# A streaming encoder layer on one core: tile 0 routed first, and the convolution shared by three engines

## The chip, the cores and the metric

The kernel runs on one core of a Trainium2 chip. The metric is the device time of one execution in microseconds (us), the median of several runs. A profiled execution is timed on its own, and its trace gives the rows below.

## What is computed

One layer over 512 prompt frames and 32 sample frames, width 1024, all in float32. The reference, cut:

```python
z = rmsnorm(x) @ w_in                       # columns: q | k | v | gate g | conv a | conv b
q, k = rotary(q), rotary(k)                 # 4 heads of 128
o, state = retention(q, k, v, state)        # decayed scores, running state
y_ret = silu(g) * groupnorm(o)
u = a * sigmoid(b)
c = depthwise_conv31(concat(conv_buf, u))   # 512 channels, 31 taps
y_conv = silu(layernorm(c))
x = x + concat(y_ret, y_conv) @ w_out
h = rmsnorm(x)
for head in range(8):                       # product-key experts
    s = (h @ query) @ keys                  # 2 x 128 scores
    e, best = top16_of_sums(top16(s1), top16(s2))
    x += sum_k softmax(best)[k] * gelu(h . down[e_k]) * up[e_k]
y = rmsnorm(x)
```

## The kernel before

**Tiles.** The 544 frames are five tiles: 0 to 3 of 128 prompt frames, tile 4 the 32 sample frames (`SAMPLE`). The kernel has a front (norm, projections, convolution, retention, output projection) and then the expert stage. In that stage each of 34 units (a tile and a head; `vt`) gathers 16 rows per frame: one gather brings 128 rows of 8 KB, 1.05 MB, into one of 11 slots. VectorE multiplies the first half with the frame and sums (`weigh`), ScalarE makes the gelu, the weight and a diagonal matrix of it, and PE adds diagonal times second half into PSUM (`sum_up`); four rows form a group, so `sums(vt, g)` are 16 matmul instructions. When PE has used a slot, the next gather may fill it. There are 34 x 16 = 544 gathers.

**Where the slots lie.** The 11 slots share their memory with the ring of three weight sections (512 columns each) and with `z`, which holds the projections. So a slot opens only when the weights or rows in it are no longer needed.

**Names of PE's jobs.** Q(t), K(t), V(t), G(t): projection of tile t on queries, keys, values, gate (`qkvg`), 16 matmul instructions at 128x512 each. `glu`: the two halves of the convolution's input, channels on partitions, four chunks of 128 channels. `head(t)`: transposes of the rotated q and k (`ret_qT`, `ret_kT`). `scores(t)`: q times k. `out(t)`, `state(t)`: scores times values, and the new state. `back(t)`: transpose of the normed result (`ret_yT`). `ln_mean`, `ln_var`: channel sums of the convolution for its layer norm. `mix_out(t, i)`: half i of the output projection. `ffn_t`, `query`, `keys`: transposes, query and key product of head 0. The lists `JOBS` and `TRANSITION` are PE's order, written out by hand; each job takes the next PSUM bank, and the engine that empties it counts on a semaphore.

**The other engines** run lists in program order too. An instruction that waits holds all behind it on its engine. On VectorE (line L728) the convolution is 31 rounds, one per tap, over four channel chunks, with one instruction for 512 prompt frames and one for 32 sample frames each, and a drain behind each round:

```python
for src, lo, n in ((u_p, 0, SEQ), (u_s, SEQ, DEC)):
    out = conv[:, c, lo:lo + n]
    ...
            last = v.scalar_tensor_tensor(out=out, in0=src[:, c, j:j + n], scalar=tap, in1=out,
                                          op0=ALU.mult, op1=ALU.add)
```

GpSimd makes the rotary (L441 to L444: 12 operations of 256 columns per tile), the decayed keys (L451), the inverse roots of the norms (L408, L414; `retention_root(t)` is the one that the retention norm of tile t needs) and issues the gathers (L465):

```python
mixed_root(0)
mixed_root(1)
pool.wait_ge(s_idx, 1)
gathers(0, 0, 3)
mixed_root(2)
pool.wait_ge(s_wsec, len(WEIGHT_ORDER) - 2)
gathers(0, 3, 7)
mixed_root(3)
pool.wait_ge(s_wsec, len(WEIGHT_ORDER))
gathers(0, 7, SLOTS)
```

SyncE's queue loads inputs, weight sections (2 MB each) and head weights, and stores the results.

## Time and profile before

| | |
|---|---|
| Median of 3 runs (lowest, highest) | 1795.74 us (1795.22, 1797.34) |
| Profiled execution | 1796.54 us, span 1794.6 us |
| PE busy | 1522.6 us, 85% |
| VectorE (DVE) busy | 1171.6 us, 65% |
| GpSimd (POOL) busy | 744.8 us, 42% |
| ScalarE (ACT) busy | 496.4 us, 28% |
| Gathers' queue | 570.46 MB, 77.1% of 16 DMA engines' span |

The span is the time from the first to the last instruction. Busy shares are means over the front and the expert stage, which have different limits, so they are read by stretches below. PE executes each float32 matmul as two rows of the trace.

### The profile page before, as it was taken

How to read it: one execution, taken by the hardware profiler on the slowest of the kernel's cores; microseconds unless marked ns; L12 is line 12 of the kernel's file. 1: busy time of each engine (PE TensorE's matmuls, PEld its weight loads, DVE VectorE, ACT ScalarE, POOL GpSimd, SP SyncE). 2: the span in 40 equal slices, each digit the busy share in tenths (PEclk: the TensorE clock that was granted, in tenths of full speed). 3: DMA queues.
4: the chain of work that ended last, by engine and by line, in shares of the span. 5: the costliest groups of instructions: out<-in, count | busy, mean ns of one | idle time of the engine just before them, and what ended most of it. 6: DMA issues, size and time to landing. Idle time of an engine off the chain costs nothing.

```text
span 1794.6 us, 14135 instructions
## 1 busy us (share of the span) xinstructions
PE 1522.6 (85%) x4008; PEld 700.3 (39%) x4008; DVE 1171.6 (65%) x2667; ACT 496.4 (28%) x1562; POOL 744.8 (42%) x654
## 2 busy tenths in 40 slices
PE   7999979968988978997798889788977988777887
PEld 3544345534433433342244334333423443332332
DVE  2089863357567767766766777677677677777655
ACT  1000110122332333332333323333333332333332
POOL 1002144133254545453554544444454445455452
PEclk9899989989999999998999999999999999899899
DMA  5112100288999999999999999999999999999996
GB/s 221 47 58 83 62 1 1 68 341 329 362 404 421 421 421 421 422 421 422 421 402 423 422 420 401 422 421 389 408 422 421 421 421 422 421 421 410 421 416 248
DMA packets 84847, 605.53 MB, mean 337 GB/s; under 512 B 10880, under 2 KB 11136, under 8 KB 13088
## 3 DMA queue, kind: packets, MB, share of 16 engines
q0 software_dynamic: 78336, 570.46, 77.1%
q1 hardware_dynamic: 6432, 34.16, 5.0%
q8 instruction: 32, 0.52, 0.1%
q14 instruction: 47, 0.39, 0.1%
HBM read 601.31 MB, written 2.88 MB: 337 GB/s over the span
## 4 chain that ended last, share of the span: by engine, by line
DMA 39%; PE 38%; DVE 13%; ACT 4%; issue 2%; POOL 1%; DVEq 1%; ACTq 1%; POOLq 0%; SPq 0%
DMA arena<-experts,expert 38%; PE ps L1246 21%; DVE region_b L728 6%; PE ps L1217 5%; PE ps L1090 5%; DVE arena L933 5%; PE ps L1077 3%; ACT weight L623 2%; ACT diag L630 1%; PE ps L1082 1%; PE ps L1189 1%; POOL arena L465 1%; PE ps L1104 1%; ACT gl L620 1%; ACTq L625 1%
## 5 line engine op out<-in xcount | busy, mean ns | idle before, releaser
L1246 PE MATMUL ps<-arena,diag 128*128 128x512 f32 x2176 | 1031.2, 631 | 234.1 <-ACT diag L630 233.9
L465 POOL DMA_INDIRECT arena<-experts,expert x544 | 669.3, 1230 | 760.3 <-PE ps L1246 672.4
L933 DVE CUSTOM_DVE_ANT_0 arena<-arena,hn 128x1024 f32<-128x1024 f32 x544 | 654.8, 1222 | 365.9 <-DMA arena<-experts,expert 361.4
L1246 PEld LDWEIGHTS ps<-arena,diag 128*128 128x128 f32 x2176 | 428.8, 201 | 818.9 <-issue 603.4
L620 ACT ACTIVATE gl<-dots 128x4 f32<-128x4 f32 x136 | 27.9, 205 | 801.4 <-DVE dots L933 801.4
L630 ACT ACTIVATE diag<-cst,weight 128x128 f32<-128x128 f32 x544 | 173.8, 390 | 9.6 <-issue 0.3
L1090 PE MATMUL ps<-arena,hT 128*128 128x512 f32 (+1 forms) x320 | 145.9, 616 | 1.0 <-issue 1.0
L623 ACT ACTIVATE weight<-gl,gate 128x1 f32<-128x1 f32 x544 | 115.8, 283 | 9.9 <-issue 0.7
L728 DVE SCALAR_TENSOR_TENSOR region_b<-region_b,par 128x512 f32<-128x512 f32 x240 | 108.0, 521 | 2.7 <-issue 0.5
L1217 PE MATMUL ps<-hT,region_b 128*128 128x512 f32 x224 | 98.5, 593 | 0.4 <-issue 0.4
L441 POOL TENSOR_TENSOR hn<-arena,cst 128x256 f32<-128x256 f32 (+1 forms) x20 | 16.2, 808 | 193.5 <-ACT arena L529 127.0
L1090 PEld LDWEIGHTS ps<-arena,hT 128*128 128x128 f32 (+1 forms) x320 | 56.9, 181 | 86.8 <-issue 86.8
L1090 PE MATMUL ps<-arena,region_b 128*128 128x512 f32 (+1 forms) x160 | 70.5, 594 | 0.0
L1217 PEld LDWEIGHTS ps<-hT,region_b 128*128 128x128 f32 x224 | 42.5, 190 | 53.5 <-issue 53.5
L1077 PE MATMUL ps<-hT,arena 128*128 128x512 f32 x128 | 58.5, 619 | 2.8 <-DVE hT L707 2.5
L713 DVE SCALAR_TENSOR_TENSOR region_b<-region_b 128x512 f32<-128x512 f32 x4 | 2.5, 686 | 75.8 <-ACT region_b L517 75.8
L944 DVE TENSOR_TENSOR xs<-ps,xs 128x1024 f32<-128x1024 f32 (+1 forms) x34 | 41.4, 1219 | 15.3 <-PE ps L1246 15.3
L933 DVE DVE_READ_ACCUMULATOR2_ANT dots<- 128x1 f32 x544 | 44.5, 82 | 0.0
L620 ACT ACT_TABLE_LOAD x34 | 43.6, 1283 | 0.6
L606 ACT ACT_TABLE_LOAD x33 | 42.3, 1283 | 1.7
L1090 PEld LDWEIGHTS ps<-arena,region_b 128*128 128x128 f32 (+1 forms) x160 | 27.0, 174 | 36.8 <-issue 36.5
L529 ACT ACTIVATE arena<-ps 128x512 f32<-128x512 f32 (+1 forms) x15 | 8.9, 595 | 110.7 <-PE ps L1090 110.7
...
## 6 DMA issues: line engine op xcount, KB each, us to landing
arena<-weights SPq DMA_DIRECT2D x8, 2048.0 KB, 8.9
region_b<-head_weights SPq DMA_DIRECT2D x8, 1152.0 KB, 9.4
arena<-experts,expert POOLq DMA_INDIRECT x544, 14.9
...
```

Source lines behind the costliest of these rows:

```text
L465: pool.indirect_dma_start(rows_of(n), None, experts, bass.IndirectOffsetOnAxis(ap=expert[:, vt % BUFS, k:k + 1], axis=0))\
L606: nc.scalar.activation(gate[:, u, :], best_s[:, u, :], ACT.Exp, bias=neg_max[:, u:u + 1], accum_out=gate_sum[:, u:u + 1]).then_inc(s_exp, 1)
L620: nc.scalar.activation(gl[:, vt % 2, ks], dots[:, vt % 2, ks], ACT.Gelu_apprx_tanh)
L623: nc.scalar.activation(weight[:, vt % 2, k:k + 1], gl[:, vt % 2, k:k + 1], ACT.Copy, scale=gate[:, vt % BUFS, k:k + 1])
L630: nc.scalar.activation(diag[:, n % DIAGS, :], base, ACT.Copy, scale=weight[:, vt % 2, k:k + 1])\
L728: last = v.scalar_tensor_tensor(out=out, in0=src[:, c, j:j + n], scalar=tap, in1=out, op0=ALU.mult, op1=ALU.add)
L933: last = v.tensor_tensor_reduce(out=rows_of(n)[:, 0:D], in0=rows_of(n)[:, 0:D], in1=hn[:, tile_of(vt)], scale=1.0, scalar=0.0, op0=ALU.mul ...
L944: v.tensor_tensor(out=xs[0:rows, tile], in0=total, in1=xs[0:rows, tile], op=ALU.add).then_inc(s_acc, 1)
L1077: last = mm(out, w[:, k, c * P:(c + 1) * P], hT[:, k, 0:SEQ], start=k == 0, stop=k == KD - 1)
L1090: last = mm(out[0:r, :], lhs[:, k, lo:lo + r], w[:, k, :], start=k == 0, stop=k == KD - 1)
L1217: last = mm(out, weights[:, k, i * KEYS:(i + 1) * KEYS], hT[:, k, 0:SEQ], start=k == 0, stop=k == KD - 1)
L1246: last = mm(ps[:, 2 * (vt % 2) + half, :], diag[:, n % DIAGS, :], rows_of(n)[:, D + half * SEC:D + (half + 1) * SEC], start=k == 0, stop=k ...
```

## The change

1. **PE's order** is one list (`plan()`). Q comes first, then GLU in 16 halves of 272 frames. Tile 0 is taken through keys, gate, values, retention and output projection ahead of the others; values, retention and output projections of tiles 1 to 4 stand between tile 0's expert work.
2. **Convolution.** Prompt and sample frames lie in one row of 574 columns per channel chunk (`WIDE`), so a tap is one instruction. VectorE does chunks 0 and 1 in 31 rounds, then tile 0's gate and scores, then chunk 2. Chunk 3 (`POOLED`) is done by ScalarE (`products`: input times tap, three buffers) and GpSimd (`tap_sums`: 30 additions).
3. **Rotary** works in place on q and k together, 6 operations of 512 columns per tile.
4. **Layer norm** of the convolution in two blocks, frames 0 to 127 first. Copies of the retention's transposes move from VectorE to ScalarE.
5. **Gathers** of unit 0 are issued one by one as memory comes free, with a slot table (`SLOT`); the first slots are reused before the others are free. Eight PSUM banks in place of seven.

```diff
-WEIGHT_ORDER = [S_A, S_B, S_Q, S_K, S_G, S_V, S_OUT, S_OUT + 1]
+WEIGHT_ORDER = [S_Q, S_A, S_B, S_K, S_G, S_V, S_OUT, S_OUT + 1]
...
+    order = turn("norm_t", 0) + turn("norm_t", 1) + rows(S_Q, 0) + turn("norm_t", 2) + rows(S_Q, 1)
+    order += turn("norm_t", 3) + rows(S_Q, 2) + turn("norm_t", SAMPLE) + rows(S_Q, 3, SAMPLE)
+    order += [("glu", s, c, i) for s in (S_A, S_B) for c in range(CT) for i in range(2)]
+    order += rows(S_K, 0) + rows(S_G, 0) + rows(S_V, 0) + head(0) + rows(S_K, 1) + scores(0) + rows(S_K, 2) + out(0)
+    order += rows(S_K, 3, SAMPLE) + rows(S_G, 1) + back(0) + rows(S_G, 2) + blocks("ln_mean") + rows(S_G, 3)
+    order += blocks("ln_var") + rows(S_G, SAMPLE) + mix(0, 0) + mix(0, 1) + rows(S_V, 1) + head(1) + turn("ffn_t", 0)
+    order += scores(1) + query(0) + keys(0) + out(1) + rows(S_V, 2, 3, SAMPLE) + back(1) + head(2) + mix(1, 0)
+    order += scores(2) + mix(1, 1) + out(2) + head(3) + back(2) + scores(3) + turn("ffn_t", 1) + out(3) + query(1)
+    order += sums(0, 0) + keys(1) + head(4) + back(3) + scores(4) + mix(2, 0) + out(4) + mix(2, 1) + back(4)
+    order += mix(3, 0) + sums(0, 1) + turn("ffn_t", 2) + mix(3, 1) + query(2) + mix(4, 0) + keys(2) + turn("ffn_t", 3)
+    order += sums(0, 2) + mix(4, 1) + query(3) + sums(0, 3) + keys(3) + turn("ffn_t", 4) + sums(1, 0) + query(4)
+    return order + sums(1, 1) + keys(4)
...
+OPENING = [0, 1, 2, 3, 4, 5, 6, 0, 1, 2, 3, 7, 8, 9, 10]
+CYCLE = [4, 5, 6, 0, 1, 2, 3, 7, 8, 9, 10]
+SLOT = OPENING + [CYCLE[n % SLOTS] for n in range(VT * TOPK - len(OPENING))]
```

SyncE's queue, the part with the output weights:

```diff
+            sp.wait_ge(s_pe, JOB[("qkvg", S_K, SAMPLE)] + 1)
+            weight_rows(S_OUT)
+            sp.wait_ge(s_convout, 32)
+            sp.wait_ge(s_conv, 1)
+            sp.wait_ge(s_pooled, TAPS - 1)
             sp.dma_start(head_flat[0], head_weights[0]).then_inc(s_hw[0], 16)
+            sp.wait_ge(s_pe, JOB[("qkvg", S_G, SAMPLE)] + 1)
+            weight_rows(S_OUT + 1)
+            sp.wait_ge(s_rot, TILES)
+            sp.dma_start(first_gain, gain_ffn.to_broadcast([P, D])).then_inc(s_gain1, 16)
+            sp.wait_ge(s_yconv, len(BLOCKS))
```

GpSimd:

```diff
+            def tap_sums(lo, hi):
+
+                for j in range(lo, hi):
+                    pool.wait_ge(s_product, j)
+                    if j == 1:
+                        pool.wait_ge(s_tap, 1)
+                    else:
+                        pool.wait_ge(s_pooled, j - 1)
+                    nc.gpsimd.tensor_tensor(out=conv[:, POOLED, :], in0=conv[:, POOLED, :],
+                                            in1=tap_product[:, j % TEMPS, :], op=ALU.add).then_inc(s_pooled, 1)
...
+            pool.wait_ge(s_cst, 16)
+            tap_sums(1, 7)
+            rotary(0)
+            decayed_keys(0)
+            tap_sums(7, TAPS)
+            retention_root(0)
+            rotary(1)
+            decayed_keys(1)
+            for t in range(2, TILES):
+                rotary(t)
 
...
             mixed_root(0)
+            pool.wait_ge(s_idx, 1)
+            pool.wait_ge(s_gate, TILES)
+            gathers(0, 0, 1)
+            retention_root(1)
+            decayed_keys(2)
+            pool.wait_ge(s_pe, JOB[("qkvg", S_V, SAMPLE)] + 1)
+            gathers(0, 1, 3)
+            pool.wait_ge(s_pe, JOB[("ret_yT", 1)] + 1)
+            gathers(0, 3, 4)
             mixed_root(1)
-            pool.wait_ge(s_idx, 1)
-            gathers(0, 0, 3)
+            retention_root(2)
+            decayed_keys(3)
+            pool.wait_ge(s_pe, JOB[("ret_yT", 2)] + 1)
+            gathers(0, 4, 5)
+            retention_root(3)
+            decayed_keys(4)
+            pool.wait_ge(s_pe, JOB[("ret_yT", 3)] + 1)
+            gathers(0, 5, 6)
+            retention_root(4)
             mixed_root(2)
-            pool.wait_ge(s_wsec, len(WEIGHT_ORDER) - 2)
-            gathers(0, 3, 7)
+            pool.wait_ge(s_pe, JOB[("ret_yT", 4)] + 1)
+            gathers(0, 6, 11)
             mixed_root(3)
-            pool.wait_ge(s_wsec, len(WEIGHT_ORDER))
-            gathers(0, 7, SLOTS)
+            pool.wait_ge(s_pe, JOB[("mix_out", SAMPLE, 0)] + 1)
```

ScalarE:

```diff
+            def products(lo, hi):
+                for j in range(lo, hi):
+                    if j > TEMPS:
+                        act.wait_ge(s_pooled, j - TEMPS)
+                    tap = G_TAPS + POOLED * TAPS + j
+                    nc.scalar.activation(tap_product[:, j % TEMPS, :], u[:, POOLED, j:j + WIDE], ACT.Copy,
+                                         scale=par[:, tap:tap + 1]).then_inc(s_product, 1)
...
+            act.wait_ge(s_u, 1)
+            products(1, 6)
+            rows_in(S_K, 0)
+            products(6, 10)
+            rows_in(S_G, 0)
+            products(10, 14)
             rows_in(S_V, 0)
-            act.wait_ge(s_by["dve"], EMPTIED[("ln_mean", 1)])
-            for c in range(CT):
-                nc.scalar.activation(yT[:, HEADS + c, :], conv[:, c, :], ACT.Square).then_inc(s_csq, 1)
-            rows_in(S_V, 1)
-            act.wait_ge(s_by["dve"], EMPTIED[("ln_var", 1)])
-            nc.scalar.activation(deviation, var[:, :], ACT.Sqrt).then_inc(s_dev, 1)
-            rows_in(S_V, 2)
-            act.wait_ge(s_yh, 1)
-            for c in range(CT):
-                nc.scalar.activation(yT[:, HEADS + c, :], conv[:, c, :], ACT.Tanh).then_inc(s_yt, 1)
-            rows_in(S_V, 3)
-            rows_in(S_V, 4)
+            turned_heads(0)
+            products(14, 18)
```

VectorE:

```diff
+            dve.wait_ge(s_st, 32)
+            dve.drain()
+            glu(0)
+            glu(1)
+            dve.drain()
+            for j in range(TAPS):
+                for c in range(2):
+                    tap(c, j)
+                if j == 11:
+                    glu(2)
+                    glu(POOLED).then_inc(s_u, 1)
+                dve.drain()
+                if j == 11:
+                    tap(POOLED, 0).then_inc(s_tap, 1)
+            gated(0)
             dve.wait_ge(s_cst, 16)
-            for name in retention_schedule():
-                if name == ("ln_mean", 0):
-                    mean_off()
-                elif name[0] == "mix_out":
-                    mix_add(*name[1:])
-                elif name == ("ln_var", 0):
-                    variance()
-                elif name[0].startswith("ret_"):
-                    ret_step(*name)
-                    if name == ("ret_scores", 0):
-                        conv_norm()
-                    elif name == ("ret_yT", 0):
-                        conv_silu()
+            ret_scores(0)
+            for j in range(TAPS):
...
+            ret_state(3)
+
+            gate_scales(0)
+            weigh(0, 0)
             first_scores(1)
             top_first(1)
+            ret_scores(4)
+            top_second(1)
+            mix_add(2, 0)
+            ret_out(4)
+            ret_state(4)
+            top_sums(1)
+            mix_add(2, 1)
+            mix_add(3, 0)
+            weigh(0, 1)
             peer_norm(2)
             mix_add(3, 1)
-            top_second(1)
-            mix_add(4, 1)
-            top_sums(1)
+            mix_add(4, 0)
+            weigh(0, 2)
             peer_norm(3)
```

**The order on GpSimd**, from behind the five roots of the first norm on. Before, each tile has four times L441, L442, L444 for its rotary and then L451 for its decayed keys; the last of tile 0 and the first of tile 1:

```order
L441 TENSOR_TENSOR hn<-arena,cst 128x4x64
L442 TENSOR_TENSOR rot_tmp<-arena,cst 128x256
L444 TENSOR_TENSOR hn<-hn,rot_tmp 128x4x64
L451 TENSOR_TENSOR hn<-hn,cst 128x512
L441 TENSOR_TENSOR hn<-arena,cst 128x4x64
```

Now, from the same place as tile 0's rotary on:

```order
L458 TENSOR_TENSOR region_b<-region_b,late 128x574 x6
L469 TENSOR_TENSOR rot_tmp<-arena,cst 128x512
L470 TENSOR_TENSOR hn<-arena,cst 128x512
L472 TENSOR_TENSOR arena<-arena,cst 128x8x64
L473 TENSOR_TENSOR arena<-arena,cst 128x8x64
L475 TENSOR_TENSOR arena<-arena,rot_tmp 128x8x64
L476 TENSOR_TENSOR arena<-arena,hn 128x8x64
L485 TENSOR_TENSOR hn<-arena,cst 128x512
L458 TENSOR_TENSOR region_b<-region_b,late 128x574 x24
L435 TENSOR_SCALAR ret_rstd<-mv 128x4
L441 TENSOR_TENSOR ret_rstd<-ret_rstd,neg_half 128x4
```

Six additions of the convolution stand ahead of tile 0's rotary (L469 to L476), 24 behind its decayed keys (L485), and the root of tile 0's retention norm (L435, L441) behind those.

**The order on VectorE**, at the end of the convolution. Before (L728 taps, L737 gate, L745 the mean taken off, L788 to L792 copies of `head(0)`):

```order
L728 SCALAR_TENSOR_TENSOR region_b<-region_b,par 128x512
L728 SCALAR_TENSOR_TENSOR region_b<-region_b,par 128x32
L737 SCALAR_TENSOR_TENSOR arena<-region_b,arena 128x512 x4
L737 SCALAR_TENSOR_TENSOR arena<-region_b,arena 32x512
L745 TENSOR_TENSOR region_b<-region_b,ps 128x4x512
L745 TENSOR_TENSOR region_b<-region_b,ps 128x4x32
L788 COPY hn<-ps 128x512
L789 TENSOR_TENSOR hn<-ps,cst 128x512
L792 COPY hn<-ps 128x512
```

Now (L877 taps, L883 gate, L947 the scores of tile 0, L955 to L966 `ret_out(0)`, L976 `ret_state(0)`, L895 the mean taken off):

```order
L875 TENSOR_SCALAR region_b<-region_b,par 128x574
L877 SCALAR_TENSOR_TENSOR region_b<-region_b,par 128x574 x38
L883 SCALAR_TENSOR_TENSOR arena<-arena 128x512
L947 TENSOR_TENSOR hn<-ps,cst 128x512
L875 TENSOR_SCALAR region_b<-region_b,par 128x574
L877 SCALAR_TENSOR_TENSOR region_b<-region_b,par 128x574 x12
L955 BN_STATS bn<-ps 128x6 x4
L958 BN_AGGR mv<-bn 128x2 x4
L962 TENSOR_SCALAR hn<-ps,mv,ret_rstd 128x128 x4
L966 TENSOR_TENSOR hn<-hn,arena 128x512
L976 COPY state<-ps 128x512
L877 SCALAR_TENSOR_TENSOR region_b<-region_b,par 128x574 x18
```

The scores and the retention norm of tile 0 have moved into the convolution, between chunks 0 and 1 and the rest of chunk 2. The 38 taps of the second row are those that stand between the first tap of chunk 3 and the scores.

**The order on PE**, around the last output projections. Before (L1090 `mix_out`, L1059 `ffn_t`, L1189 `query`, L1201 `keys`, L1246 `sums`):

```order
L1090 MATMUL ps<-arena,region_b 128x512 x8
L1201 MATMUL ps<-region_b,cst 128x128 x2
L1090 MATMUL ps<-arena,region_b 128x512 x8
L1090 MATMUL ps<-arena,region_b 32x512 x8
L1059 MATMUL ps<-cst,hn 128x128 x8
L1189 MATMUL ps<-hT,region_b 128x128 x16
L1246 MATMUL ps<-arena,diag 128x512 x8
L1201 MATMUL ps<-region_b,cst 128x128 x2
L1059 MATMUL ps<-cst,hn 128x128 x8
L1246 MATMUL ps<-arena,diag 128x512 x8
```

Now (L1276 `mix_out`, L1406 `sums`, L1258 `back(4)` and `ffn_t`, L1346 `query`, L1359 `keys`):

```order
L1276 MATMUL ps<-arena,region_b 128x512 x8
L1406 MATMUL ps<-arena,late 128x512 x8
L1258 MATMUL ps<-cst,hn 128x128 x8
L1276 MATMUL ps<-arena,region_b 128x512 x8
L1346 MATMUL ps<-hT,region_b 128x128 x16
L1276 MATMUL ps<-arena,region_b 32x512 x8
L1359 MATMUL ps<-region_b,late 128x128 x2
L1258 MATMUL ps<-cst,hn 128x128 x8
L1406 MATMUL ps<-arena,late 128x512 x8
L1276 MATMUL ps<-arena,region_b 32x512 x8
```

The weighted sums and two more tiles' turns have moved ahead of the last output projection, the second row of `32x512`.

## Rows read from the trace of the kernel before

**Rows 1.** Stretches, us: PE, PEld, DVE, ACT, POOL busy, PEclk, DMA share, GB/s.

```profile
340.00:380.00 40.00, 37.61 (x148) 18.60 (x146) 22.46 (x72) 5.70 (x14) 13.63 (x15) 1.00 0.58 223
380.00:420.00 40.00, 23.58 (x76) 12.75 (x76) 26.56 (x64) 9.27 (x30) 9.48 (x10) 0.79 0.70 265
420.00:460.00 40.00, 34.88 (x112) 17.85 (x112) 27.81 (x66) 16.63 (x56) 15.30 (x16) 0.96 1.01 412
460.00:500.00 40.00, 39.94 (x131) 20.84 (x131) 15.62 (x27) 10.38 (x33) 12.79 (x13) 1.00 0.89 340
500.00:1000.00 500.00, 421.35 (x1041) 189.05 (x1041) 353.23 (x823) 161.18 (x531) 244.44 (x196) 0.96 1.01 419
```

**Rows 2.** Timeline of PE and GpSimd: start, us, engine, line, instructions, idle before.

```profile
339.05 0.61 PE L1201 MATMUL ps<-region_b,cst 128*128 128x128 f32 x4
...
353.18 1.20 POOL L465 DMA_INDIRECT arena<-experts,expert  x1 [28.62 <-DVE expert L918]
...
374.04 1.02 POOL L465 DMA_INDIRECT arena<-experts,expert  x1 [4.42 <-PEq L1157]
```

**Rows 3.** Chain of waits: start us, us, what.

```profile
19.07 27.73 PE ps L1077 x64
...
94.84 0.69 DVE region_b L713
...
211.06 6.21 PE ps L1104 x16
...
218.17 6.87 PE ps L1090 x16
...
359.85 13.87 PE ps L1090 x32
```

**Rows 4.** The page, DMA issues: count, KB each, median us to landing.

```profile
arena<-weights SPq DMA_DIRECT2D x8, 2048.0 KB, 8.9
region_b<-head_weights SPq DMA_DIRECT2D x8, 1152.0 KB, 9.4
```

**Rows 5.** Chain of waits, the convolution while GpSimd works and after.

```profile
139.89 4.41 DVE region_b L728 x6
...
146.12 4.40 DVE region_b L728 x6
...
152.34 3.26 DVE region_b L728 x6
...
156.58 2.48 DVE region_b L728 x6
...
160.04 2.48 DVE region_b L728 x6
```

**Rows 6.** Timeline of VectorE: a dependent pair, and `ret_out(0)`.

```profile
234.52 0.72 DVE L758 TENSOR_TENSOR region_b<-region_b 128x544 f32<-128x544 f32 x1
235.32 0.72 DVE L760 TENSOR_TENSOR region_b<-region_b,var 128x544 f32<-128x544 f32 x1
...
243.64 0.88 DVE L799 BATCH_NORM_STATS2 bn<-ps 128x6 f32<-128x128 f32 x4
...
247.85 0.74 DVE L810 TENSOR_TENSOR hn<-hn,arena 128x512 f32<-128x512 f32 x1
```

**Rows 7.** Timeline of GpSimd: 512 columns beside the convolution and without it.

```profile
152.53 1.37 POOL L451 TENSOR_TENSOR hn<-hn,cst 128x512 f32<-128x512 f32 x1 [0.24 <-issue]
...
246.33 1.04 POOL L451 TENSOR_TENSOR hn<-hn,cst 128x512 f32<-128x512 f32 x1
```

**Rows 8.** Timeline: VectorE's first products, ScalarE and PE behind them.

```profile
381.31 1.21 DVE L933 CUSTOM_DVE_ANT_0 arena<-arena,hn 128x1024 f32<-128x1024 f32 x1
...
385.99 0.21 ACT L620 ACTIVATE gl<-dots 128x4 f32<-128x4 f32 x1 [2.97 <-DVE dots L933]
...
387.73 9.77 PE L1246 MATMUL ps<-arena,diag 128*128 128x512 f32 x16 [8.12 <-ACT diag L630]
```

**Rows 9.** Gathers from 340 to 500 us, from issue to landing.

```profile
DMA to landing us min/median/max: 5.4/9.0/13.3
```

750 lines of the change are left out of this document (420 added, 330 removed).

## The prediction

> **What bounds the kernel now.** I read the stretches first [rows 1]. From 500 us on the core moves 419 GB/s, nearly all of it expert rows, with its DMA engines full. Only the front can be changed here, and all it can change is when that flow starts. Then GpSimd's line [rows 2]: the first gather is issued at 353.2 us, and the slots under the last weights open at 374.0 us, released by PE. That is the end of `mix_out(4,1)`, the last output projection. I call this moment M: from it on all 11 slots serve the gathers. The chain of waits [rows 3] shows what sets M: VectorE starts the convolution at 94.8 us, PE gets its result at 211.1 us, and from there PE works nearly without a gap. One product (16 rows of the trace at 128x512) takes 6.87 us.
>
> **What a later M costs.** From 340 to 500 us the core moves 40 us x (223+265+412+340) GB/s = 49.6 MB [rows 1]. Less two head weights (1.18 MB each [rows 4]), three copies of 128 KB and a gain of 512 KB, that is 46.3 MB, or 44 gathers of 1.05 MB. In the changed kernel 13 gathers are issued before M: 11 have landed, two go with `mix_out(4,0)` and land about M. Behind M it moves 412 GB/s, less the same 3.3 MB and the same 2.9 MB by which 460 to 500 us falls short (PE is full there). So by 500 us it has 13 + ((498 - M) x 0.412 - 6.2) / 1.05 gathers. That equals 44 at M = 404. Each us past 404 costs 1 us, each us before gains 1.
>
> **Up to the convolution.** Queries now go first on PE (5 x 6.87 us), then 16 GLU halves of 272 columns. At 272/512 of a product each is 3.65 us, 58.4 us together, against 75 us before (19.1 us, to just before VectorE's 94.8 [rows 3]). Tile 0's transposes no longer wait for the identity as long, so I start the queries at 12 us. The halves of the first two chunks are ready at about 96 us: VectorE starts where it did. PE is through the GLU at 112 us.
>
> **The convolution on VectorE.** It was 31 rounds of 8 instructions, 3.46 us a round [rows 5]. Now an instruction covers 574 columns. A dependent pair at 544 columns starts 0.80 us apart [rows 6], which makes 0.83 us for a tap with its drain and 0.665 us for one with none. Two chunks make 1.50 us a round, the third alone 0.83 us: 31 x 2.33 = 72 us instead of 107. Chunk 3 goes to ScalarE (a product) and GpSimd (30 adds).
>
> **The toll.** GpSimd's tensor_tensor and VectorE's taps, both with two inputs in SBUF, hold each other up. While GpSimd did tile 0's rotary, a round took 6.23 us instead of 3.46 us [rows 5]: 2.77 us for six operations of 256 columns, 0.46 us each. One operation of 512 columns cost 3.26 - 2.48 = 0.78 us. On that line 574 columns cost 0.86 us. GpSimd is itself slowed, from 1.04 to 1.37 us at 512 columns [rows 7]; alone, 574 columns take 1.11 us. Work it through:
> - 96.5 to 118.5: two GLU products, 12 rounds of 1.50, two more GLU products, first tap of chunk 3. GpSimd may now start.
> - 38 taps stand ahead of `ret_scores(0)`: 25.3 us. In that time GpSimd does 6 adds, 6 rotary operations, the decayed keys and 19 adds: 25 x 0.86 + 7 x 0.78 = 27 us of toll. With gated(0) and the scores themselves: 173.8 us.
> - PE goes on from 112 with K(0), G(0), V(0), 6.87 us each, stands 3 us for the rotary and 2 us for ScalarE's copies, and is done with K(2) at 154.5. Next in line is `out(0)`, which needs those scores. It stands 19 us. Queued behind it is K(3); ScalarE's products 26 to 30 are queued behind the copy of K(3), and GpSimd's last five adds behind them. After `out(0)`, `state(0)` and K(3) on a slow clock, K(3) is there at 186.5, the adds end at 193.5.
> - VectorE stops after 13 taps of chunk 2 (184) in `ret_out(0)`, for a root that GpSimd computes only behind all 30 adds: 195. The rest of `ret_out` (4.9 us in all [rows 6]) ends about 198.
> - 18 taps remain. GpSimd now does the rotary of tiles 1 to 4, 25 operations in a row. One tap per operation, each 0.665 + 0.78: about 25 us. The convolution ends at 223 us; before it was 211.
>
> The bounds: with no toll at all the same walk gives 147 us for the scores, 167 for the root and 185 for the end. With 1.11 us per add (the add's whole length) it ends at about 232.
> The Trainium skill (SBUF — State Buffer, "SBUF: two separate sides") calls this an exclusive lock held for the whole instruction. By that rule the end is the 232 of the upper bound and the time 9 us above my forecast; the trace agrees on who blocks whom, but shows 0.78 us of toll for an operation that alone takes 1.04 us [rows 5, 7]. The Trainium skill (Perfetto Trace Analysis, "Optimizing Scalar/DVE Operations") also warns that moving work between these two engines might not help, which speaks against this change.
>
> **From the sums to M.** From `ln_mean` the statistics, root, norm and tanh of block 0 pass between four engines for 24 us, covered by G(3) and G(4) on PE: `mix_out(0,0)` starts at 247. PE's time goes with columns (0.43 us for a row of 512, a quarter of that for 128). Behind the start of `mix_out(0,0)`, up to M, PE has 9 output projections and `mix_out(0,0)` itself (10 x 6.87 = 68.7), four V products (27.5), retention of tiles 1 to 4 (44 rows of 128 columns each: 19), the turns of four tiles (3.6), three queries (10.5), keys (1.5) and three weighted sums (20.6): 151 us. The sums, two of the turns and one query were behind M before; the GLU's 17 us less are taken off ahead of the convolution, where VectorE's line hides them. Waits of PE that I find in the order:
> - `mix_out(0,1)` for its weights, loaded only after G(4) (8.9 us to land [rows 4]): 2.5.
> - copies and `back(2)`, `ffn_t(1)`: about 10.
> - `sums(0,0)`: VectorE begins its four products after `ret_out(3)`, 4.6 us [rows 8], and the four diagonals follow: 8.
> - `sums(0,1)`: its products are queued behind the add of `mix_out(3,0)`, PE's preceding job. So PE stands while VectorE and ScalarE do theirs: 7.
> - `ffn_t(3)`: its norm is behind products that need gather 11, which waits for `mix_out(4,0)` and takes 5.4 us at best to land [rows 9]: 8.
> After such a wait the clock is at its 1.2 GHz level: 16 matmuls took 9.77 us instead of 6.87 behind an 8.1 us wait [rows 8], at a mean clock of 0.79 in that stretch [rows 1]. Three times: 7.5. In all 247 + 151 + 35.5 + 7.5 = 441; the walk is good to a few us, and I take M = 438. Routing on tile 0 takes 14.1 us from its keys to the gather [rows 2]; here the keys come at 279, and the first gather at about 290.
>
> **The sum.** 438 - 404 = 34 us later. The profiled execution took 1796.54 us (span 1794.6 and 1.9 around it), 0.8 above the median of 1795.74. So 1830 us.
>
> **Rivals.**
> - *No toll* (0.12). The adds are long and dependent, and taps might slip between them for free. For it: the walk's toll at 574 columns is a line drawn through two widths. Against it: both widths in [rows 5] cost VectorE. `ln_mean` is then at 185 instead of 223, M = 400, 1792 us: a hair on the faster side. From `ln_mean` at 189 on, M is back at 404.
> - *PE stays fed behind the convolution* (0.12), the one that ends on the other side. VectorE and ScalarE run ahead of PE there, so that the 35.5 us of waits and their 7.5 us of slow clock are not paid: M = 395 in spite of the toll, 1787 us. It decides where less than 9 of these 43 us are left. For it: VectorE's own work between 247 and M is well under PE's. Against it: the products of `sums(0,1)` are queued behind an add that itself waits for PE's preceding job, whoever is ahead.
> - *Half the toll* (0.06): `ln_mean` at 200, and M at 408 to 415: 1800 to 1807 us.
> - *Worse* (0.06): the whole instruction blocks; `ln_mean` 9 us later again and a slow clock behind each longer wait bring it past 1850, to 1865.
> - *The walk* (0.64): 1805 to 1850, for 25 us less or 20 us more waiting than I found.
>
> **Chances.** A measurement of this kernel can tell 0.2%, 3.6 us, from no change. Faster: all of the fed PE and two thirds of no toll, 0.20. Same: the other third of no toll and half of the half toll, 0.07. Slower: 0.64 + 0.06 + 0.03 = 0.73. The range 1786 to 1850 leaves out the worse case and the low half of the fed PE, 0.12, and some 0.05 of the walk; the walk's own range is 1805 to 1850.
>
> **What would show it.** Right: VectorE's taps near 1.5 us apart while GpSimd adds; PE idle some 19 us before the first scores-times-values product; a pause of 10 us in VectorE's line before `ret_out(0)`'s subtraction; `ln_mean` at 223; first gather near 290, but the flow at 419 GB/s only from about 440. PE waits of 7 to 8 us before the three weighted sums or their neighbours. Wrong: taps at 0.8 us throughout, `ln_mean` before 189, or M before 404.

## The result

The changed kernel takes 1858.62 us (median of 4 runs, 1853.94 to 1860.26), the kernel before 1795.51 us beside it: a ratio of 1.0345, 95% interval 1.0323 to 1.0367. The forecast was 1830 us in a range of 1786 to 1850: the direction was right, the size was not. The profiled execution is the fastest of the four (1853.94 us, span 1852.1 us), 57.5 us above the span before; what follows accounts for that one.

The stretches of the changed kernel, columns as in [rows 1]:

```profile
340.00:380.00 40.00, 32.28 (x142) 18.16 (x142) 18.27 (x67) 5.98 (x18) 4.54 (x6) 0.91 0.08 27
380.00:420.00 40.00, 29.67 (x95) 15.09 (x94) 12.36 (x25) 6.54 (x19) 6.93 (x9) 0.87 0.37 144
420.00:460.00 40.00, 26.37 (x64) 9.59 (x63) 8.45 (x19) 3.80 (x12) 5.70 (x2) 0.79 0.15 53
460.00:500.00 40.00, 23.81 (x97) 13.94 (x96) 24.98 (x59) 9.98 (x29) 20.81 (x20) 0.83 0.96 371
500.00:1000.00 500.00, 437.54 (x1064) 196.93 (x1064) 342.61 (x793) 160.09 (x525) 231.37 (x189) 0.94 1.00 412
```

From 500 us on, the flow is nearly what it was: 412 GB/s and a DMA share of 1.00 against 419 and 1.01 [rows 1]. Between 340 and 500 us the core moves 40 us x (27+144+53+371) GB/s = 23.8 MB, where it moved 49.6 MB. The missing 25.8 MB at 0.412 MB per us are 63 us. Against them stand the gathers that now come early: from 240 to 340 us the core moves 84 GB/s x 100 us = 8.4 MB, before 1.8. Up to 240 us it is 1.4 MB behind, and from 500 to 1000 us 3.5. In all 24.1 MB are missing at 1000 us, which at 0.417 MB per us are 58 us, the whole loss. So the place is in the main the front, as forecast, and the loss is larger than forecast.

VectorE's timeline of the changed kernel (start, us, engine, line, instructions) shows the convolution while GpSimd adds, and its last 18 taps beside the rotary:

```profile
97.70 17.72 DVE L877 SCALAR_TENSOR_TENSOR region_b<-region_b,par 128x574 f32<-128x574 f32 x22
...
117.76 60.29 DVE L877 SCALAR_TENSOR_TENSOR region_b<-region_b,par 128x574 f32<-128x574 f32 x38
...
179.99 10.62 DVE L877 SCALAR_TENSOR_TENSOR region_b<-region_b,par 128x574 f32<-128x574 f32 x12
...
199.43 1.36 DVE L962 TENSOR_SCALAR hn<-ps,mv,ret_rstd 128x128 f32<-128x128 f32 x4 [7.41 <-POOL ret_rstd L441]
...
202.93 30.48 DVE L877 SCALAR_TENSOR_TENSOR region_b<-region_b,par 128x574 f32<-128x574 f32 x18
```

22 taps without GpSimd took 17.7 us, which is 1.61 us for a round of two taps and a drain; the 38 beside it, 19 rounds, took 60.3, which is 3.17 a round. The first 12 taps of chunk 2 after the one that starts it, each with its drain and with nothing beside them, took 10.6 us, 0.89 each. The pause ahead of `ret_out(0)`'s subtraction (line 962) is 7.4 us (10 forecast), and the last 18 taps took 30.5 us (25 forecast). PE's timeline, with its idle time in brackets:

```profile
179.48 2.08 PE L1313 MATMUL ps<-arena,hn 128*128 128x128 f32 x8 [21.73 <-DVE hn L947]
...
233.47 5.94 PE L1285 MATMUL ps<-region_b,ones_cw 128*128 128x128 f32 x16 [22.27 <-DVE region_b L877]
...
256.88 7.13 PE L1276 MATMUL ps<-arena,region_b 128*128 128x512 f32 x16
...
353.17 8.83 PE L1406 MATMUL ps<-arena,late 128*128 128x512 f32 x16 [7.72 <-ACT late L755]
...
399.63 9.50 PE L1406 MATMUL ps<-arena,late 128*128 128x512 f32 x16 [10.33 <-ACT late L755]
...
439.53 1.97 PE L1258 MATMUL ps<-cst,hn 128*128 128x128 f32 x8 [11.46 <-DVE hn L1035]
443.67 9.66 PE L1406 MATMUL ps<-arena,late 128*128 128x512 f32 x16 [2.17 <-ACT late L755]
453.26 7.05 PE L1276 MATMUL ps<-arena,region_b 128*32 128x512 f32 x16
...
477.82 9.66 PE L1406 MATMUL ps<-arena,late 128*128 128x512 f32 x16 [13.73 <-ACT late L755]
```

`ln_mean` starts at 233.5 (223 forecast), `mix_out(0,0)` at 256.9 (247), and M, the end of `mix_out(4,1)`, is 453.26 + 7.05 = 460.3 (438). The waits stand where they were looked for: 7.7 us ahead of `sums(0,0)`, 10.3 ahead of `sums(0,1)`, 11.5 ahead of `ffn_t(3)`. After M comes one that was not in the forecast, 13.7 us ahead of `sums(0,3)`. GpSimd's timeline says why:

```profile
296.78 1.20 POOL L513 DMA_INDIRECT arena<-experts,expert  x1 [22.23 <-DVE expert L1100]
...
387.84 1.06 POOL L513 DMA_INDIRECT arena<-experts,expert  x1 [0.16 <-issue]
...
427.71 4.75 POOL L513 DMA_INDIRECT arena<-experts,expert  x1 [8.00 <-PE ps L1276]
432.76 0.95 POOL L513 DMA_INDIRECT arena<-experts,expert  x1 [0.30 <-issue]
462.30 0.18 POOL L435 TENSOR_SCALAR rstd<-sq_sum 32x1 f32<-32x1 f32 x1 [28.59 <-ACT hn L560]
462.57 0.56 POOL L441 TENSOR_TENSOR rstd<-rstd,neg_half 32x1 f32<-32x1 f32 x1
463.31 1.02 POOL L513 DMA_INDIRECT arena<-experts,expert  x1 [0.18 <-issue]
```

The first gather goes out at 296.8 (290 forecast, [rows 2] 353.2). From 433.7 to 462.3 GpSimd stands at the root for tile 4's norm, whose square ScalarE can do only behind `mix_out(4,1)`. Gather 13, whose slot is open at 460.3, is queued behind this root and leaves at 463.3.

### The profile page after: what moved, and what is told of

It is laid out like the page before. It is cut to its first block, busy times and chain, and to the rows that moved or that the text cites. A ratio compares the mean times of both kernels' runs of the same rounds, so it can differ in the third digit from the quotient of the medians.

```text
span 1852.1 us, 14121 instructions
## 1 busy us (share of the span) xinstructions
PE 1529.5 (83%) x4008; PEld 718.0 (39%) x4008; DVE 1173.5 (63%) x2509; ACT 530.4 (29%) x1633; POOL 788.4 (43%) x654
## 4 chain that ended last, share of the span: by engine, by line
PE 40%; DMA 39%; DVE 10%; ACT 4%; DVEq 2%; issue 2%; POOL 1%; ACTq 1%; POOLq 0%; SPq 0%
DMA arena<-experts,expert 38%; PE ps L1406 22%; PE ps L1276 7%; PE ps L1374 5%; DVE arena L1115 4%; DVE region_b L877 4%; PE ps L1269 2%; DVEq L1001 2%; ACT weight L748 2%; ACT late L755 1%; DMA arena<-weights 1%; POOL arena L513 1%; PE ps L1258 1%; PE ps L1346 1%; ACT gl L745 1%
## 5 line engine op out<-in xcount | busy, mean ns | idle before, releaser
L1406 PE MATMUL ps<-arena,late 128*128 128x512 f32 x2176 | 1053.2, 642 | 233.1 <-ACT late L755 232.8
L1406 PEld LDWEIGHTS ps<-arena,late 128*128 128x128 f32 x2176 | 437.6, 205 | 831.9 <-issue 611.6
L745 ACT ACTIVATE gl<-dots 128x4 f32<-128x4 f32 x136 | 27.9, 205 | 812.1 <-DVE dots L1115 812.0
L755 ACT ACTIVATE late<-cst,weight 128x128 f32<-128x128 f32 x544 | 173.8, 390 | 9.4
L1276 PE MATMUL ps<-arena,hT 128*128 128x512 f32 (+1 forms) x320 | 143.9, 606 | 0.2 <-DMA arena<-weights 0.2
L748 ACT ACTIVATE weight<-gl,gate 128x1 f32<-128x1 f32 x544 | 115.8, 283 | 10.5 <-issue 1.4
L877 DVE SCALAR_TENSOR_TENSOR region_b<-region_b,par 128x574 f32<-128x574 f32 x90 | 114.9, 1304 | 4.3
L458 POOL TENSOR_TENSOR region_b<-region_b,late 128x574 f32<-128x574 f32 x30 | 46.5, 1550 | 120.5 <-DVE region_b L875 98.9
L1276 PEld LDWEIGHTS ps<-arena,hT 128*128 128x128 f32 (+1 forms) x320 | 56.1, 179 | 80.4 <-issue 80.3
L1276 PE MATMUL ps<-arena,region_b 128*128 128x512 f32 (+1 forms) x160 | 70.9, 596 | 1.0 <-DMA arena<-weights 0.6
L435 POOL TENSOR_SCALAR rstd<-sq_sum 128x1 f32<-128x1 f32 (+1 forms) x15 | 4.7, 311 | 146.7 <-ACT hn L560 146.4
L1269 PE MATMUL ps<-hT,arena 128*128 128x272 f32 x256 | 58.9, 393 | 0.0
L988 DVE TENSOR_TENSOR xs<-ps,xs 128x512 f32<-128x512 f32 (+1 forms) x10 | 6.9, 688 | 82.2 <-PE ps L1276 82.2
L1269 PEld LDWEIGHTS ps<-hT,arena 128*128 128x128 f32 x256 | 48.6, 190 | 10.8 <-issue 0.8
```

The lines of the kernel that those rows point to most:

```text
L458: nc.gpsimd.tensor_tensor(out=conv[:, POOLED, :], in0=conv[:, POOLED, :], in1=tap_product[:, j % TEMPS, :], op=ALU.add).then_inc(s_pooled, 1)
L745: nc.scalar.activation(gl[:, vt % 2, ks], dots[:, vt % 2, ks], ACT.Gelu_apprx_tanh)
L748: nc.scalar.activation(weight[:, vt % 2, k:k + 1], gl[:, vt % 2, k:k + 1], ACT.Copy, scale=gate[:, vt % BUFS, k:k + 1])
L755: nc.scalar.activation(diag[:, n % DIAGS, :], base, ACT.Copy, scale=weight[:, vt % 2, k:k + 1])\
L877: return v.scalar_tensor_tensor(out=conv[:, c, :], in0=u[:, c, j:j + WIDE], scalar=gain, in1=conv[:, c, :], op0=ALU.mult, op1=ALU.add)
L1269: last = mm(out[:, 0:HALF], w[:, k, c * P:(c + 1) * P], hT[:, k, i * HALF:(i + 1) * HALF], start=k == 0, stop=k == KD - 1)
```

## Experiments

"By 520" below counts the gathers issued between 280 and 520 us; one carries 1.05 MB, 2.5 us of the flow at 0.417 MB per us. It is a rough measure. Ratios are to the kernel before, which ran beside each. The span is that of the profiled execution.

| kernel | `ln_mean` us | M us | by 520 | span us | median us | ratio (95%) |
|---|---|---|---|---|---|---|
| before | 211.1 | 373.7 | 56 | 1794.6 | 1795.51 | |
| changed | 233.5 | 460.3 | 35 | 1852.1 | 1858.62 | 1.0345 (1.0323 to 1.0367) |
| a1 adds of one column | 206.8 | 435.3 | 40 | 1828.2 | 1832.78 | 1.0205 (1.0183 to 1.0227) |
| a2 rotary behind | 219.1 | 457.9 | 35 | 1849.6 | 1850.97 | 1.0302 (1.0284 to 1.0321) |
| a3 outputs first | 233.7 | 410.2 | 43 | 1822.0 | 1830.43 | 1.0213 (1.0171 to 1.0255) |
| a4 gathers before roots | 233.8 | 410.6 | 40 | 1830.5 | 1832.29 | 1.0217 (1.0189 to 1.0244) |
| a5 drained products | 234.9 | 415.6 | 39 | 1841.1 | 1842.33 | 1.0260 (1.0242 to 1.0277) |
| a6 all on VectorE | 221.4 | 450.1 | 38 | 1842.6 | 1842.28 | 1.0260 (1.0233 to 1.0287) |
| a7 a4 and a6 together | 220.9 | 395.8 | 46 | 1817.8 | 1820.28 | 1.0141 (1.0120 to 1.0162) |
| b1 halves and 574 columns | 191.8 | 352.3 | 65 | 1770.9 | 1775.06 | 0.9881 (0.9863 to 0.9899) |
| b2 halves only | 195.5 | 355.2 | 63 | 1776.2 | 1778.21 | 0.9902 (0.9885 to 0.9918) |
| b3 574 columns only | 208.6 | 368.0 | 59 | 1787.4 | 1792.01 | 0.9975 (0.9966 to 0.9985) |

**a1: the toll of the adds.** GpSimd's adds of chunk 3 cover one column instead of 574, so chunk 3 is not summed.

```diff
-nc.gpsimd.tensor_tensor(out=conv[:, POOLED, :], in0=conv[:, POOLED, :],
-                        in1=tap_product[:, j % TEMPS, :], op=ALU.add)
+nc.gpsimd.tensor_tensor(out=conv[:, POOLED, 0:1], in0=conv[:, POOLED, 0:1],
+                        in1=tap_product[:, j % TEMPS, 0:1], op=ALU.add)
```

> The changed kernel, with each of GpSimd's 30 adds of chunk 3 cut from 574 columns to 1 (so chunk 3 of the convolution is not summed; all else is computed). ScalarE's products stay. Theory (the toll): the adds hold up VectorE's taps. In the changed kernel two taps and a drain take 3.46 us while GpSimd adds, 1.50 us by the uncontended rows. Then the 38 taps ahead of the first scores take about 32 us instead of 60, PE's 21.7 us idle ahead of the first scores-times-values product nearly goes, ln_mean is at 190 to 200 instead of 233.5, M (the end of the last output projection) at 418 to 427 instead of 460, and the time is 33 to 43 us shorter: 1815 to 1825 us. Rival 1 (ScalarE's products are what slows VectorE, not the adds): taps stay at 1.7 us each, ln_mean near 230, time within 5 us of 1858. Rival 2 (the front of the convolution is not what sets the end; the wait is for a transfer or a weight section further on): ln_mean early, M at 450 or later, time above 1848.

Its VectorE timeline:

```profile
97.23 17.72 DVE L877 SCALAR_TENSOR_TENSOR region_b<-region_b,par 128x574 f32<-128x574 f32 x22
...
117.31 36.99 DVE L877 SCALAR_TENSOR_TENSOR region_b<-region_b,par 128x574 f32<-128x574 f32 x38
...
176.28 30.49 DVE L877 SCALAR_TENSOR_TENSOR region_b<-region_b,par 128x574 f32<-128x574 f32 x18
```

The same 38 taps take 37.0 us, 23.3 less for the 25 adds beside them: 0.93 us an add, where the forecast had 0.86. At the pace of the 22 taps ahead of them, 1.61 us a round, the 38 would take 30.6; the 6.4 us more are 0.91 for each of the seven operations of tile 0's rotary and keys, and nothing is left for the adds of one column. The last 18 taps, beside the rotary, stay at 30.5. `ln_mean` comes 26.7 us earlier and M 25.0, and the span is 23.9 us shorter. Rivals 1 and 2 fall: ScalarE's products go on as before and cost nothing that can be seen, and what the front gains arrives at the end. But `ln_mean` (206.8), M (435.3) and the time all came later than I expected (190 to 200, 418 to 427, 1815 to 1825 us): I let the adds pay for tolls that the seven operations of tile 0's rotary cause.

**a2: the toll of the rotary, moved.**

```diff
             retention_root(0)
+            pool.wait_ge(s_conv, 1)
             rotary(1)
```

> The changed kernel, with one wait more on GpSimd: the rotary of tiles 1 to 4 (and the decayed keys of tile 1) begins when VectorE's last tap is done. Theory (the toll of GpSimd's two-input operations, a whole operation each): the last 18 taps take 18 x 0.83 = 15 us instead of 30.5, ln_mean comes at 218 instead of 233.5; the 25 rotary operations then take 25 x 1.25 = 31 us behind it, up to 250, before the transposes of tile 1 need them (about 262), but they now stand beside the statistics of block 0 on VectorE and may take back 3 to 6 us there. M at 448 to 452 instead of 460, time 1846 to 1851 us. Rival (what VectorE pays to GpSimd in the last 18 taps is only handed on, since the operations between the mean and the tanh pay the same): time within 3 us of 1858.

VectorE's timeline, the taps and then block 0's norm; below it the same norm in a1, where the rotary is over:

```profile
203.09 15.96 DVE L878 SCALAR_TENSOR_TENSOR region_b<-region_b,par 128x574 f32<-128x574 f32 x18
...
238.08 1.40 DVE L913 TENSOR_TENSOR region_b<-region_b 128x128 f32<-128x128 f32 x1
...
242.16 1.40 DVE L919 TENSOR_TENSOR var<-region_b 128x128 f32<-128x128 f32 x1
...
245.31 3.80 DVE L928 TENSOR_SCALAR region_b<-region_b,half_ln 128x128 f32<-128x128 f32 x4
```

```profile
225.68 0.29 DVE L912 TENSOR_TENSOR region_b<-region_b 128x128 f32<-128x128 f32 x1
...
226.72 0.29 DVE L918 TENSOR_TENSOR var<-region_b 128x128 f32<-128x128 f32 x1
...
227.86 1.11 DVE L927 TENSOR_SCALAR region_b<-region_b,half_ln 128x128 f32<-128x128 f32 x4
```

The 18 taps need 16.0 us, `ln_mean` is at 219.1 as expected, and then the toll is paid again: an instruction of 128 columns takes 1.40 us instead of 0.29, four `tensor_scalar` 3.80 instead of 1.11. Of 14.4 us at `ln_mean`, 2.4 are left at M and 2.5 in the span. The medians lie 7.7 us apart, which puts the time at the upper edge of what the theory expected (1846 to 1851), while M (457.9, expected 448 to 452) and the span speak for the rival: most of what is spared in the taps is handed on. How much of the time is saved, 2.5 or 7.7 us, stays open. The short instructions also tell what the toll goes by: VectorE pays about the length of one GpSimd operation for an instruction of its own, short or long, while GpSimd's operations follow one another.

**a3: the outputs first.** The front stays; PE's order, and VectorE's and GpSimd's with it, changes behind `mix(3, 0)`:

```diff
-order += mix(3, 0) + sums(0, 1) + turn("ffn_t", 2) + mix(3, 1) + query(2) + mix(4, 0) + keys(2) + turn("ffn_t", 3)
-order += sums(0, 2) + mix(4, 1) + query(3) + ...
+order += mix(3, 0) + mix(3, 1) + mix(4, 0) + mix(4, 1) + sums(0, 1) + turn("ffn_t", 2) + query(2) + keys(2)
+order += turn("ffn_t", 3) + sums(0, 2) + query(3) + ...
```

and on GpSimd, without its waits:

```diff
-mixed_root(2); gathers(0, 6, 11); mixed_root(3); gathers(0, 11, 13); mixed_root(SAMPLE); gathers(0, 13, TOPK)
+gathers(0, 6, 11); mixed_root(2); gathers(0, 11, 13); gathers(0, 13, TOPK); mixed_root(3); mixed_root(SAMPLE)
```

> The changed kernel with another order behind the output projection of tile 3's first half: PE does the other three output projections (mix_out(3,1), (4,0), (4,1)) before the second weighted sums of tile 0, the turns and queries of tiles 2 and 3; VectorE's adds and GpSimd's gathers follow that order, and GpSimd issues gathers before the roots of tiles 2 to 4. The front is untouched. Theory (only M counts, 1 us per us; the front's late end is one part of it and PE's waits for its own gathers and norms the other): ahead of M stand 24 us less of PE's work (two weighted sums 13.8, two turns 1.8, a query and keys 3.9, and their slow clock), and the waits of 10.3 and 11.5 us are behind M. M at 410 to 420 instead of 460, the flow at 412 to 419 GB/s from there, time 1806 to 1820 us. Rival (the early weighted sums and queries are needed early: VectorE and PE then starve behind M, and the flow doesn't start though the slots are open): M at 410 to 420 but the time above 1840 us.

GpSimd's timeline:

```profile
410.50 11.61 POOL L513 DMA_INDIRECT arena<-experts,expert  x1 [4.59 <-PE ps L1276]
422.42 0.95 POOL L513 DMA_INDIRECT arena<-experts,expert  x1 [0.30 <-issue]
...
438.23 0.86 POOL L435 TENSOR_SCALAR rstd<-sq_sum 32x1 f32<-32x1 f32 x1 [8.15 <-ACT hn L560]
...
440.78 1.45 POOL L513 DMA_INDIRECT arena<-experts,expert  x1 [0.18 <-issue]
```

M is at 410.2, 50 us earlier, but the time is 28 us shorter (30 by the spans), between theory and rival. With the slots open at 410, gather 13's issue takes 11.6 us, and from 424.6 GpSimd stands at the roots of tiles 3 and 4; full flow begins at 440.8. That is 22.5 us ahead of the changed kernel's 463.3, and three more gathers (13 to 15) have gone out by then, 2.5 us each: together 30 us, which is the difference of the spans. So M alone does not set the time; in a3 the moment from which GpSimd issues without a stop does. Before, the two fell together (373.7 and 374.0). The medians are less sure than the others: a3's runs lie between 1823.8 and 1843.6 us.

**a4: the queue behind M.** a3 with another order on GpSimd (its wait for tile 1's indices and the rest of the loop left out here):

```diff
             gathers(0, 13, TOPK)
             mixed_root(3)
+            gathers(1, 0, 8)
             mixed_root(SAMPLE)
+            gathers(1, 8, TOPK)
```

> The kernel with the outputs first, and one more move on GpSimd: gathers 0 to 7 of tile 1 now stand ahead of the root of tile 4's squares (and behind that of tile 3's). In the outputs-first run M was at 410 as expected, but GpSimd issued gather 13 of tile 0 in 11.6 us instead of 0.95 (410.5 to 422.1, as long as VectorE's products ran without a gap), and stood from 424.6 at the roots of tiles 3 and 4 until 440.6, for squares that ScalarE does behind the diagonals; the flow was full from 441 only. Theory (the flow starts when the slots are open and GpSimd's queue has come to gathers whose indices are ready; M is only the first of the two): the next gathers go out at about 430 to 431, behind the root of tile 3, 10 us earlier, the flow is full from there, and the span is 7 to 11 us shorter than the 1822.0 of the outputs-first kernel: 1811 to 1815, time about 1815 to 1822. Rival (what is missing behind M is work of PE and VectorE on landed rows: the slots are given back too slowly, so earlier issues only land earlier): span within 3 us of 1822.

It came out 8.5 us worse than a3 by the span; the medians are within 2 us. The next gathers do leave at 430.6, as the theory had it. But the root is now behind gathers that wait for PE's sums. VectorE's timeline shows who waits for it:

```profile
458.50 1.27 DVE L1038 SCALAR_TENSOR_TENSOR hn<-xs,rstd,region_b 32x1024 f32<-32x1024 f32 x1 [15.63 <-POOL rstd L441]
```

VectorE stands 15.6 us at tile 4's norm, and its products of tile 1 are queued behind. Theory and rival both missed by their numbers: issues were early, but each slot is given back only by sums that wait for that norm. In substance this is near the rival, which had the slots given back too slowly.

**a5: gaps between the products.** In a4, gather 13's issue took 11.6 us again. a5 is a4 with `dve.drain()` ahead of each product in `weigh`.

> The same kernel as the run before this one, and a drain on VectorE ahead of each of its products of a gathered row with the normed row. Theory (GpSimd's issue of a gather stands for as long as VectorE's products follow each other without a gap, and a gap lets it through): gather 13 of tile 0, which took 11.6 us in the outputs-first run and 4.75 us in the changed kernel, takes 1 to 2.5 us; gathers 14 and 15 go out some 8 us earlier and the span is up to 5 us shorter than without the drains. Rival (the gap of a drain is too short, or the issue stands for another reason, such as descriptors of earlier gathers): gather 13 takes 9 us or more again, and the span is the same or 1 to 3 us longer, for 528 drains more.

GpSimd's issue of gather 13 in this kernel, and VectorE's products beside it:

```profile
415.88 0.94 POOL L513 DMA_INDIRECT arena<-experts,expert  x1 [4.59 <-PE ps L1280]
417.12 1.37 POOL L513 DMA_INDIRECT arena<-experts,expert  x1 [0.30 <-issue]
```

```profile
416.45 1.23 DVE L1119 CUSTOM_DVE_ANT_0 arena<-arena,hn 128x1024 f32<-128x1024 f32 x1
...
417.80 1.23 DVE L1119 CUSTOM_DVE_ANT_0 arena<-arena,hn 128x1024 f32<-128x1024 f32 x1
...
419.15 1.23 DVE L1119 CUSTOM_DVE_ANT_0 arena<-arena,hn 128x1024 f32<-128x1024 f32 x1
```

The issue takes 0.94 us, as the theory said, and the next one 1.37, with products 1.35 us apart instead of 1.15. Yet the span is 10.6 us longer than a4's (median 10.0), not shorter. M is 5 us later; where the other half goes was not traced. There was little to gain: of a3's and a4's 544 issues only this one took over 2.1 us, and of the changed kernel's only gather 11's.

**a6 and a7: the offload undone.** Without ScalarE's products and GpSimd's adds; VectorE takes chunk 3's taps itself:

```diff
             for j in range(TAPS):
                 for c in range(2):
                     tap(c, j)
+                if j >= 12:
+                    tap(POOLED, j - 12)
...
+            for j in range(TAPS - 12, TAPS):
+                tap(POOLED, j)
+                tap(2, j - (TAPS - 12))
+                dve.drain()
```

> The changed kernel with the offload alone undone: ScalarE's 30 products and GpSimd's 30 adds of chunk 3 are gone, and VectorE does all four chunks, in instructions of 574 columns as before (three taps a round from tap 12 on, then 12 rounds with chunk 2's first taps, then its last 19 with tile 0's retention behind seven of them). Order on PE, rotary and all behind stay. Theory (an add on GpSimd holds VectorE up by about 1.0 us, more than the 0.665 us that VectorE needs for the tap itself): 124 taps and 50 drains take 93 us without toll, plus 2 GLU products behind the first, the seven operations of tile 0's rotary and keys (7 us), retention 8 us, and some of tile 1 to 4's rotary; first scores at about 183 and ln_mean at 214 to 224 instead of 233.5. M 10 to 19 us earlier, time 1841 to 1850. Rival (the offload does pay for itself, and the 1.0 us is only what the three engines' handing over costs): ln_mean at 233 or later, 1858 or more.

> Both repairs together: the convolution all on VectorE, the outputs first, and gathers ahead of the root of tile 4. Theory: the parts add, since each us that ln_mean comes earlier moves all behind it: M at 393 to 401, time 8 to 18 us below that of the gathers-before-roots kernel, 1800 to 1812 us; it stays above the kernel before (1796) and far above the one that has only the convolution's new form (1775), because the early routing of tile 0 puts 20 to 25 us of PE's waits and extra work ahead of M. Rival (the order with tile 0 first is good once its front is not late): below 1790.

a6: `ln_mean` at 221.4, M 10.2 us and the span 9.5 us earlier, the median 16 us: the offload costs more than it saves, its rival falls. All of this is within what was expected. a7: M is at 395.8, as expected, but it takes 1820 us and not 1800 to 1812. It beats a4 by 12 us, within the 8 to 18 expected, so the parts do add. That the rest of the miss is a4's own loss is likely, but was not run.

**b1, b2, b3: two other parts of the change alone, in the order of before.** The convolution's core in b1 and b3, condensed:

```diff
-for src, lo, n in ((u_p, 0, SEQ), (u_s, SEQ, DEC)):
-    v.scalar_tensor_tensor(out=conv[:, c, lo:lo + n], in0=src[:, c, j:j + n], ...)
+v.scalar_tensor_tensor(out=conv[:, c, :], in0=u[:, c, j:j + WIDE], ...)
```

and PE's in b1 and b2, condensed:

```diff
-for c in range(CT):
-    for k in range(KD): mm(out, w[:, k, c * P:(c + 1) * P], hT[:, k, 0:SEQ], ...)
-for c in range(CT):
-    for k in range(KD): mm(out[:, c * DEC:(c + 1) * DEC], ..., hT[:, k, SEQ:T], ...)
+for c in range(CT):
+    for i in range(2):
+        for k in range(KD): mm(out[:, 0:HALF], ..., hT[:, k, i * HALF:(i + 1) * HALF], ...)
```

> The kernel before, with two parts of the change alone: the GLU products in halves of 272 columns, and the convolution with prompt and sample in one instruction of 574 columns, all four chunks on VectorE. Order, rotary, retention and everything behind stay as before; nothing goes to GpSimd or ScalarE. Theory: PE's GLU takes 58.4 us instead of 75, VectorE starts at about 78, a round of four taps takes 4 x 0.665 + 0.17 = 2.83 us instead of 3.46, and with the toll of tile 0's rotary the convolution ends at about 78 + 4 + 88 + 12 = 182; PE is at the end of its V product at about 192 instead of 209 and now sets ln_mean: 17 to 19 us earlier. M at 355 to 358 instead of 374, first gather 335. One us per us: 1777 to 1782 us. Rival 1 (before M=374 nothing is gained by being earlier, because the expert flow is then held by VectorE's routing or the head weights' transfers): 1790 to 1796. Rival 2 (it is the layout of 574 columns that is slow, not the adds on GpSimd): a round of four taps takes as long as before or longer, and the time is 1796 or above.

> The kernel before with the GLU products in halves alone; the convolution keeps prompt and sample in instructions apart (eight a round). Theory (ln_mean comes at the later of two ends: PE's own line of products, 191.8 us with the halves and 209 without, and VectorE's convolution): VectorE starts at about 81 and needs 115 us as in the kernel before, ending at 197 to 198, so VectorE sets it: 13 us earlier than before. M at 359 to 362, time 1780 to 1786, about 6 us above the kernel with both parts. Rival (the merged instructions bring nothing, the halves all): within 2 us of 1775.

> The kernel before with the convolution in instructions of 574 columns alone; the GLU products stay 512 columns wide with the sample's apart. Theory (the later of two ends): VectorE starts at 94.8 and is done by 195 to 197, but PE comes out of its own line of products only at 209, so ln_mean is at 209 instead of 211: 2 us, and 1792 to 1796 us. Rival (VectorE's convolution is what sets the start of all behind it, as the chain of waits of the kernel before reads): ln_mean at 197, and 1780 to 1784 us.

VectorE's convolution in b1, and PE around `ln_mean` in b1, b2 and b3 (lines 1109 and 1111):

```profile
83.18 97.83 DVE L734 SCALAR_TENSOR_TENSOR region_b<-region_b,par 128x574 f32<-128x574 f32 x120
180.94 1.28 DVE L743 SCALAR_TENSOR_TENSOR arena<-region_b,arena 128x512 f32<-128x512 f32 x2
```

```profile
184.81 7.10 PE L1094 MATMUL ps<-arena,hT 128*128 128x512 f32 x16 [0.26 <-issue]
191.75 4.41 PE L1109 MATMUL ps<-region_b,ones_cw 128*128 128x512 f32 x16
```

```profile
195.51 4.51 PE L1111 MATMUL ps<-region_b,ones_cw 128*128 128x512 f32 x16 [2.97 <-DVE region_b L736]
```

```profile
208.62 4.41 PE L1109 MATMUL ps<-region_b,ones_cw 128*128 128x512 f32 x16
```

In b1 VectorE is done at 181 and PE goes from its own product into `ln_mean` without a wait: PE sets it, as the theory had it. With halves alone PE waits 3.0 us for VectorE (195.5), with 574 columns alone PE's own products end at 208.6. b1 is 1.19% faster than the kernel before and the fastest of all: M 21.4 us earlier, the span 23.7 us shorter, both a little better than expected (M 355 to 358, 1777 to 1782 us). Its rivals fall. b2 too came out better than its theory: M 355.2 for 359 to 362, 1778.2 us for 1780 to 1786. It is 3.2 us above b1, so the 574 columns add little to the halves; its rival had asked for 2 us or less. b3's theory had the time right, but M came 5.7 us earlier for 2.5 at `ln_mean`. In all three M gains 2 to 3 us more than `ln_mean` does; that was not traced.

## Why the prediction was right and wrong

**Right: the currency.** The front decides, and a us there is a us at the end, where only the front is moved: a1 25.0 us of M for 23.9 of the span, a6 10.2 for 9.5, b1 21.4 for 23.7. By the forecast's own formula M = 460.3 with its 3 us behind it gives 463.3 - 404 = 59 us; 57.5 were measured. The "fed PE" rival fell: PE's waits from `mix_out(0,0)` to M add up to 38 us.

**Wrong in size, first: what the taps take by themselves.** The prediction works out 1.50 us for a round of two taps with its drain, and then prices "38 taps stand ahead of `ret_scores(0)`: 25.3 us", which is 38 x 0.665, without a drain. These 19 rounds do have drains, and a round with nothing beside it took 1.61 us: 30.6 us. The last 18 taps are priced at 0.665 each as well, 12.0 us; each has a drain, and a2 shows them with nothing beside them in 16.0. Together 9.3 us too little. The toll was nearly right: 60.3 - 30.6 = 29.7 us for 32 operations, 0.93 each, where 27 were forecast; and 30.5 - 16.0 = 14.5 us for the last 18 taps, 0.81 each for a forecast 0.78. That is 3.2 us too little. The rounding of 26 to 25 us adds 1.0, and smaller errors the other way take 3.0 off: `out(0)` came 5.7 us late (179.5 for 173.8), the last 18 taps began 4.9 us late (202.9 for 198) and took 5.5 us more, and `ln_mean` is 10.5 us later. (The split is by subtraction. Where VectorE stands for GpSimd, part of a drain may be hidden in that time.)

My upper bound, the add's whole length, gave 232 for an end measured at 233.5. That is luck: the bound has the same short taps in it. The Trainium skill (SBUF — State Buffer, "SBUF: two separate sides") has that rule, an exclusive lock for the whole instruction. The trace agrees that the two engines take turns. But with the taps at their measured pace the walk ends, by estimate, at about 232 with the 0.86 us of my line and at about 241 with 1.11: the cost of an add, 0.93, is nearer to the line. The line was drawn through rounds in which four of eight instructions had 32 columns [rows 5], while VectorE pays for short instructions too (a2); that this bent the line is argued, not run.

**Wrong in size, second: PE's line up to M.** From `mix_out(0,0)` it took 203.4 us against 191. The waits were 38.4 us (35.5), slow clock behind them 9 (7.5; for the three sums 8.8 to 9.7 us instead of 7.1), which leaves 156 of work against 151 counted: 5 us of gaps and short jobs. That the sum of the waits is so near is luck in part: those up to `ffn_t(1)` were 6.7 us for 12.5 forecast, the three late ones 29.5 for 23, and 2.2 ahead of `sums(0,2)` were not in the forecast. Another 3 us I took off when I wrote 438 for a sum of 441.

**Missed: GpSimd's queue.** The 3 us behind M, where gather 13 is queued behind a root; and 4.75 us for gather 11's issue beside VectorE's products, which is part of the 11.5 us ahead of `ffn_t(3)`. Together: 10.5 - 0.6 (from `ln_mean` to `mix_out(0,0)`) + 12.4 (from there to M, the 3 of 438 included) = 22.3 us of M, and 3 behind it: the 25 us between the 34 forecast and the 59 that the same formula gives.

**Which part of the change costs what.** The halves and the 574 columns are worth -21 us (b1). So the rest costs 63 + 21 = 84 us, of which undoing the offload gives back 16 (a6) by the medians and 10 by the spans. The other 68 or more, by subtraction, belong to everything else together: the order with tile 0 early, the rotary in wide operations, the norm in two blocks, the copies on ScalarE, the slot table. Of these only the end of the order was run: a3 gives back 28 us when the last three output projections go first. Where the time sits can be read from the marks: between b1 and the changed kernel `ln_mean` comes 42 us later and the way from there to M is 66 us longer. Undoing the offload returns 12 of the 42 (a6). Of the 30 left, some 16 are there when the convolution starts (96.9 us in a6, 81.1 in b1), with the queries ahead of the GLU, and 9.5 are the toll of the next tiles' rotary on the last 12 taps (20.1 us in a6, 10.6 alone). a7, with both repairs, is still 45 us above b1, and no run divides those 45.
